# Three feed-forwards rearranged: all inner tiles first, then the down projection output by output, in 512 columns

## The reference, cut to what matters

```python
# layer 0
f = (silu(h @ w_ffn_gate) * (h @ w_ffn_up)) @ w_ffn_down
x = x + rms_norm(f, post_ffn_norm)
# layers 1 and 2
h = rms_norm_2(x, ffn_norm_g[l])
x = x + (silu(h @ ffn_w_gate[l]) * (h @ ffn_w_up[l])) @ ffn_w_down[l]
# after layer 2
return rms_norm_2(x, final_norm_g)
```

## Time and profile before

| | |
|---|---|
| median of three runs | 994.09 us |
| the profiled execution, its own time | 994.75 us |
| its span, first to last instruction | 993.0 us |
| TensorE matmul busy | 982.1 us, 99% |
| VectorE busy | 727.4 us, 73% |
| ScalarE busy | 527.6 us, 53% |
| DMA | 156.64 MB, mean 158 GB/s |
| granted TensorE clock | 9 of tenths (full) in all 40 slices |

### The profile page before, as it was taken

One profiled execution on the slowest core, in us unless ns is written; L12 is line 12 of the kernel. 1 busy time (PEld: TensorE's weight loads), 2 busy tenths in 40 slices (PEclk: granted clock), 3 DMA queues, 4 the chain that ended last, 5 costly groups with the idle time before them and its releaser, 6 DMA issues.

```text
span 993.0 us, 18707 instructions
## 1 busy us (share of the span) xinstructions
PE 982.1 (99%) x7840; PEld 895.6 (90%) x7840; DVE 727.4 (73%) x1219; ACT 527.6 (53%) x787; POOL 4.2 (0%) x11
## 2 busy tenths in 40 slices
PE   9999999999999999999999999999999999999997
PEld 8998999898989988889999898998887999899997
DVE  6978688886767997857676666788877577676666
ACT  5486564545456663556455454475446455544543
POOL 1000000000000000000000000000000000000000
PEclk9999999999999999999999999999999999999999
DMA  9744534545453322313565455443221265545531
GB/s 340 197 159 158 185 133 170 202 181 212 170 194 141 127 97 88 128 43 131 186 214 203 175 182 200 170 165 117 94 101 44 84 213 171 209 172 185 197 128 43
DMA packets 24684, 156.64 MB, mean 158 GB/s; under 512 B 2720, under 2 KB 4264, under 8 KB 7064
## 3 DMA queue, kind: packets, MB, share of 16 engines
q1 hardware_dynamic: 22320, 151.64, 42.8%
q10 hardware_dynamic: 1928, 2.49, 1.1%
q0 software_dynamic: 352, 1.31, 0.4%
HBM read 153.99 MB, written 1.44 MB: 157 GB/s over the span
## 4 chain that ended last, share of the span: by engine, by line
PE 91%; DVE 4%; ACT 2%; issue 2%; DMA 1%; SPq 0%; DVEq 0%; ACTq 0%
PE bank L489 42%; PE bank L715 21%; PE bank L717 10%; PE bank L576 2%; DVE arena L1780 1%; PE bank L1009 1%; PE bank L1014 1%; ACT w_hi L1296 1%; DVE w_lo L1798 1%; PE bank L1025 1%; PE bank L581 1%; PE bank L970 1%; DMA raw<-in_w 1%; PE bank L1233 1%; PE bank L518 1%
## 5 line engine op out<-in xcount | busy, mean ns | idle before, releaser
L1798 DVE TENSOR_TENSOR w_lo<-raw,w_hi 128x2048 fp32r<-128x2048 f32 (+3 forms) x141 | 316.9, 2250 | 103.0 <-ACT w_hi L1296 102.6
L715 PE MATMUL bank<-h_both,w_hi 128*128 128x512 f32 x912 | 323.5, 399 | 1.6 <-DVE arena L1780 1.6
L1296 ACT ACTIVATE w_hi<-raw 128x2048 fp32r<-128x2048 f32 (+4 forms) x153 | 273.2, 1787 | 34.4 <-PE bank L489 27.6
L717 PE MATMUL bank<-h_both,w_lo 128*128 128x256 f32 x912 | 256.7, 281 | 0.0
L715 PEld LDWEIGHTS bank<-h_both,w_hi 128*128 128x128 f32 x912 | 171.6, 188 | 42.9 <-DVE arena L1780 2.3
L489 PE MATMUL bank<-mix_hi,w_hi 128*128 128x256 f32 x720 | 207.0, 287 | 0.0
L489 PE MATMUL bank<-mix_lo,w_hi 128*128 128x256 f32 x720 | 204.1, 284 | 0.0
L489 PE MATMUL bank<-mix_hi,w_lo 128*128 128x256 f32 x720 | 204.1, 283 | 0.0
L717 PEld LDWEIGHTS bank<-h_both,w_lo 128*128 128x128 f32 x912 | 172.8, 189 | 0.0
L489 PE MATMUL bank<-h_both,w_hi 128*128 128x256 f32 x880 | 163.9, 288 | 0.3 <-DVE w_lo L1798 0.2
L489 PEld LDWEIGHTS bank<-h_both,w_hi 128*128 128x128 f32 x880 | 137.3, 191 | 6.2 <-issue 2.1
(11 more groups left out here) (317 smaller groups left out, 1049.3 us busy)
## 6 DMA issues: line engine op xcount, KB each, us to landing
raw<-in_w SPq DMA_DIRECT2D x136, 1024.0 KB, 4.9
raw<-in_w SPq DMA_DIRECT2D x2, 896.0 KB, 4.5
raw<-in_w SPq DMA_DIRECT2D x3, 512.0 KB, 3.6
raw<-in_w SPq DMA_DIRECT2D x2, 768.0 KB, 4.2
cst<-in_consts SPq DMA_DIRECT2D x1, 1120.0 KB, 11.0
raw<-in_first SPq DMA_DIRECT2D x4, 256.0 KB, 5.1
x<-in_first SPq DMA_DIRECT2D x4, 256.0 KB, 5.3
arena<-bias_rows ACTq DMA_DIRECT2D x4, 256.0 KB, 5.5
```

What stands on the lines that cost most here:

```text
L715: pe.matmul(to, hi(k), h_both[:, :, k, :], start=(k == 0), stop=False, skip_group_check=True)
L717: last = pe.matmul(to[:, 0, :], lo(k), h_hi[:, k, :], start=False, stop=(k == KT - 1), skip_group_check=True)
L1296: return act.activation(dst, src, ACT.Copy, **kw)
L1798: dve.tensor_tensor(w_lo[:, s, 0:n], raw[:, s, 0:n], w_hi[:, s, 0:n].bitcast(F32), ALU.subtract)\
```

## The change

A feed-forward now has two parts. First all 22 inner tiles are made and their hi and lo parts kept, side by side in one buffer (`act_both`) in the arena. Then the down products come output by output: output d takes its 22 products in order. For outputs 0 to 6 each is one matmul of 512 columns and one of 256 into a bank of their own (7, 4 and 5 in turn); output 7 keeps three of 256 into bank 6. The down weights are laid out in that order, 16 tiles to a chunk. The two sums of an output are added (`output`), and the squares of an output are made and summed as soon as it is there (`squared`, `squares`). Gate and up of the wide inner tiles use banks 0 to 3 in turn. The rounding of an inner tile (`rounded`) and its rest (`rest`) come one turn later on ScalarE and VectorE than before. The angles, the Sin and the table load for Ln and Exp move into the second part; the angles' buffers move to the mixer's. Not shown below: in `normed_residual`, outputs 0 to 6 are read from SBUF (xg) and the part sums between the halves are gone; the last norm's gains go with each output; `norm_sum` takes two addends for a half in place of three or four.

```diff
@@ -97,6 +97,15 @@
 ]
+DOWNS = KT * FT // 16
+DOWN_EVENTS = sorted([(16 * i + 16, "chunk", i) for i in range(DOWNS)] + [(FT * d + FT, "tile", d) for d in range(KT)])
+DOWN_EVENTS = [event[1:] for event in DOWN_EVENTS if event[1:] not in (("chunk", DOWNS - 1), ("tile", KT - 1))]
 def stream():
     out = []
@@ -106,10 +115,8 @@
         if l:
             out += [(l, "uq", 0, 2 * 768), (l, "ukv", 0, 1024)]
         out += [(l, "out", i, CH) for i in range(4)]
-        out += [(l, "gu", 0, CH), (l, "gu", 1, CH)]
-        for p in range(1, FT // 2):
-            out += [(l, "gu", 2 * p, CH), (l, "gu", 2 * p + 1, CH), (l, "down", p - 1, CH)]
-        out.append((l, "down", FT // 2 - 1, CH))
+        out += [(l, "gu", j, CH) for j in range(FT)]
+        out += [(l, "down", i, CH) for i in range(DOWNS)]
     return out
@@ -292,7 +300,10 @@
         xo = xg.rearrange("p k t -> p (k t)").rearrange("p (h k t) -> p h k t", h=2, k=KT)
         FF, _ = area(0, dict(gu=(2, 2, T), sg=(2, T), act=(2, T), part=(2, T), sums=(2, T)))
-        act_hi, act_lo = mix_hi[:, 0:4, :], mix_lo[:, 0:4, :]
+        act_both = nc.alloc_sbuf_tensor_at("act_both", [P, 2, FT, T], F32R, offset=arena_at + 12 * T * 4)
+        act_hi, act_lo = act_both[:, 0, :, :], act_both[:, 1, :, :]
+        assert (12 + 2 * FT) * T <= ARENA - 4096
         B1, at_products = area(0, dict(
             lx=(2, 259), lg=(2, T), glr=(T,), gk=(T,), gq=(T,), gv=(TT, T), gout=(2, T), mq=(4, T), mk=(4, T),
@@ -419,18 +430,12 @@
         WIDE = range(3, FT)
-        def gate_up_turn(j):
-            return j + sum(i < j for i in WIDE)
         def gate_up_bank(j, t=0):
...
+            return pairs((2 * (j - 3) + t) % 4 if j in WIDE else (4, 5, 7)[j])
+        def fed_bank(d):
+            return pairs((7, 4, 5)[d % 3])
         def projected(l, i):
@@ -710,7 +699,8 @@
                         for t in range(2):
                             hi, lo = tile_of(c, KT, 2 * P, t * P)
                             to = gate_up_bank(j, t)
-                            pe.wait_ge(V.sem, gate_up_read(l, gate_up_turn(j) + t - 3))
+                            if j - 2 in WIDE:
+                                pe.wait_ge(V.sem, V.at(l, ("gate", "up")[t], j - 2))
                             for k in range(KT):
                                 pe.matmul(to, hi(k), h_both[:, :, k, :], start=(k == 0), stop=False,
                                           skip_group_check=True)
@@ -718,8 +708,6 @@
                                                  skip_group_check=True)
                             last.then_inc(M.sem, M.mark(l, "gu" if t else "gate", j))
                         return
-                    if j >= 3:
-                        pe.wait_ge(V.sem, gate_up_read(l, gate_up_turn(j) - 3))
                     for t in range(2):
                         if just_come and t == 0:
                             rounded_first(gate_up_bank(j)[:, t, :], c, 2 * P, 0, 2 if c in HALVED else 1)
@@ -729,40 +717,31 @@
                             norm_sum(l, "ffn")
                     last.then_inc(M.sem, M.mark(l, "gu", j))
...
+                def down():
+                    pe.wait_ge(V.sem, V.at(l, "gu", 2))
+                    for i in range(KT * FT):
+                        d, j = divmod(i, FT)
+                        c, first, end = CHUNK[l, "down", i // 16], j == 0, j == FT - 1
+                        if i % 16 == 0:
+                            split(pe, c)
+                        if d == 0:
+                            pe.wait_ge(V.sem, V.at(l, "act", "lo", j))
+                        elif first and 3 <= d < KT - 1:
+                            pe.wait_ge(V.sem, V.at(l, "fed", "read", d - 3))
+                        hi, lo = tile_of(c, 16, P, 0)
+                        if d < KT - 1:
+                            pe.matmul(fed_bank(d), hi(i % 16), act_both[:, :, j, :], start=first, stop=False,
+                                      skip_group_check=True)
+                            last = pe.matmul(fed_bank(d)[:, 0, :], lo(i % 16), act_hi[:, j, :], start=False, stop=end,
+                                             skip_group_check=True)
+                        else:
+                            last = product(out_tile(l, "fed", d), (hi, lo), [i % 16],
+                                           [lambda k, q=q: q[:, j, :] for q in (act_hi, act_lo)],
+                                           start=first, stop=end, loose=True)
+                        if end:
+                            last.then_inc(M.sem, M.mark(l, "fed", "tile", d))
+                        elif i % 16 == 15:
+                            last.then_inc(M.sem, M.mark(l, "down", i // 16))
                 c = CHUNK[l, "gu", 0]
                 pieces = [(1, gate_up_bank(0), [(c, 2 * P, 0), (c, 2 * P, P)]),
@@ -770,11 +749,9 @@
                 as_they_come(l, "ffn", pieces[:2 if l == 0 else 1])
                 if l:
                     gate_up(1)
...
+                for j in range(2, FT):
+                    gate_up(j)
+                down()
@@ -1421,40 +1398,69 @@
                         hi_of(c + RING)
                 def silu(j):
-                    if j >= 1:
-                        act.wait_ge(V.sem, V.at(l, "act", "lo", j - 1))
                     act.wait_ge(V.sem, V.at(l, "gu", j))
                     act.activation(FF["sg"][:, j % 2, :], FF["gu"][:, j % 2, 0, :], ACT.Silu)\
                         .then_inc(A.sem, A.mark(l, "silu", j))
+                def rounded(j):
                     act.wait_ge(V.sem, V.at(l, "act", j))
-                    copy(act_hi[:, j % 4, :], FF["act"][:, j % 2, :]).then_inc(A.sem, A.mark(l, "act", "hi", j))
+                    copy(act_hi[:, j, :], FF["act"][:, j % 2, :]).then_inc(A.sem, A.mark(l, "act", "hi", j))
+                def parts(j):
+                    for t in range(2):
+                        act.wait_ge(M.sem, M.at(l, "gu" if t else "gate", j))
+                        if j - 1 in WIDE:
+                            act.wait_ge(V.sem, V.at(l, ("gate", "up")[t], j - 1))
+                        copy(FF["part"][:, t, :], gate_up_bank(j, t)[:, 1, :]).then_inc(A.sem, A.mark(l, "part", t, j))
+                def output(d):
+                    if l == 0:
+                        act.wait_ge(M.sem, M.at(l, "fed", "tile", d))
+                        copy(xg[:, d, :], fed_bank(d)[:, 1, :]).then_inc(A.sem, A.mark(l, "fed", "part", d))
+                    if l == 1 and d in (2, 4, 6):
+                        hi_of_x(l + 1, "in", f"attn{l + 1}", d // 2 - 1)
+                    if l != 1 and d:
+                        squared(d - 1)
+                def squared(d):
+                    act.wait_ge(V.sem, V.at(l, "fed", "read", d))
+                    src, name = (xg, (l, "fed")) if l == 0 else (x, (LAYERS, "final"))
+                    act.activation(sq[:, d, :], src[:, d, :], ACT.Square).then_inc(A.sem, A.mark(*name, "sq", d))
                 after(c0)
                 norm_factor(l, "ffn")
                 after(c0 + 1)
...
+                for j in range(2):
+                    silu(j)
+                    rounded(j)
+                after(c0 + 2)
+                silu(2)
+                rounded(2)
+                for j in WIDE:
+                    parts(j)
+                    after(CHUNK[l, "gu", j])
+                    if j - 1 in WIDE:
+                        rounded(j - 1)
+                    silu(j)
+                rounded(FT - 1)
+                if l == 2:
+                    ln_and_exp()
+                for kind, i in DOWN_EVENTS:
+                    if kind == "tile":
+                        output(i)
+                        continue
+                    after(CHUNK[l, "down", i])
+                    if l == 0 and i == 6:
                         act.wait_ge(V.sem, V.at("angles"))
-                        for i in range(4):
-                            last = act.activation(rope[:, i, :], rope[:, i, :], ACT.Sin)
+                        for n in range(4):
+                            last = act.activation(rope[:, n, :], rope[:, n, :], ACT.Sin)
                         last.then_inc(A.sem, A.mark("rope"))
+                        ln_and_exp()
+                if l != 1:
+                    squared(KT - 2)
             def block1():
                 l, lru = 0, B1["lru"]
@@ -2388,25 +2373,48 @@
                 def added(j):
-                    after_a(l, "silu", j - 2)
-                    after_v(l, "act", j - 2)
                     for t, name in enumerate(("gate", "up")):
                         after_a(l, "part", t, j)
                         tt(FF["sums"][:, t, :], gate_up_bank(j, t)[:, 0, :], FF["part"][:, t, :], ALU.add, l, name, j)
                     after_v(l, "up", j)
+                    after_a(l, "silu", j - 2)
+                    after_v(l, "act", j - 2)
                     tt(FF["gu"][:, j % 2, :, :], FF["sums"], wide(rstd[:, :], 2), ALU.mult, l, "gu", j)
-                def feed(j):
```

(68 more changed lines are left out.)

171 lines of the change are left out of this document (26 added, 145 removed).

## The result

The changed kernel took 987.08 us (median of 6 runs, 986.06 to 988.36) against 994.19 us for the kernel before beside it (6 runs): ratio 0.9928, 95% interval 0.9919 to 0.9938. That is 7.1 us less where 5.6 were forecast, and 0.2 us under the range. The six runs form two groups: 986.20, 986.11 and 986.06, and 987.98, 988.36 and 987.96. The mean granted clock was 0.998 or 0.999 in all six, so the clock doesn't part them. The profiled execution is of the first group (986.20 us, span 984.4).

The account below looks back on a forecast made before the run. TensorE, busy 99% of the span, was taken as the bound; gains of 3.0 (down), 2.0 (layer 0's wait), 0.5 (end of layer 0) and 0.1 (last norm) sum to 5.6 us, giving 988.5 us, range 987.3 to 991.2.

Parts of the forecast that it names:

- What would show it: Signs against: wide matmuls waiting mid first part for VectorE or a lo split, output 0's last products waiting, clock leaving 1.00.
- Down products: Outputs 0 to 6: two matmuls a tile instead of three save 6.6 ns on 462 tiles, 3.0 us; bounds 0 to 3.4.
- The isolated gap's rule: Down tiles: a fixed cost of 2.5 ns per instruction, 1.2 us in all; with the pair's rival, chance together 0.06.
- The wait in layer 0: First wide tiles of layer 0: TensorE's waits for VectorE to read a bank, 2.12 us, go; 2.0 us counted as gained.
- No stall in 22 tiles in a row: Gate-up part: about 6 us of room stand ahead of any stall of the successive wide tiles: 0.
- none from inner tiles to down: Output 0 wants inner tile 21 last, with 0.8 us of room before TensorE would wait: 0.
- none in the down part: Second part: VectorE's and ScalarE's work, with the angles, Sin and table load, fits the room without stalling TensorE: 0.
- the slower rival: First part: VectorE's loop becomes longer than TensorE's 5.65 us a tile, such as 17 us lost, 1005.6 us; chance 0.05.
- The end of layer 0: Layer 0's last norm step: Ln no longer waits for VectorE's part sums, 0.5 us gained; bounds 0 and 0.6.
- The last norm: Final norm: the square of tile 7 no longer waits for VectorE's sum behind a part sum, 0.1 us gained.
- more than forecast: Case of more gain, from steps priced at nothing or a smoother first part, down to 986 us; chance 0.07.

Follow-up runs that it names:

- e3: The changed kernel with each down tile of outputs 0 to 6 made by three matmuls of 256 columns instead of one of 512 and one of 256: 991.93 us.
- e7: The changed kernel with down products of layers 0 and 2 fed from the gate and up activations instead of the kept inner tiles: 985.67 us, one execution.
- e2: The changed kernel with six banks in turn instead of four for wide gate and up, so no pause at inner tile 5 of layer 0: 987.49 us.
- e4: The changed kernel with one wait at the start of each layer's down part, for TensorE's own last gate-up product: 987.09 us.

## Why the prediction missed, step by step

Two terms failed: the price of a down pair, and the first part of layer 0, which was priced at one pace for its row. None of the signs under "What would show it" that would make the forecast wrong came, and yet the time left the range.

**Down products.** Right in mechanism, mis-sized by a third: 6.6 ns a tile forecast, 8.7 to 9.0 measured (0.3597 to 0.3510; e3 0.3600), 4.0 to 4.1 us and not 3.0. The term failed in taking 0.3534 us, the price of a gate-up pair in one stretch, for the down pair, which takes 0.3510; e7 shows that the operand makes the difference. The step said that its operand lies in another buffer, but used that for the lower bound only; it put an upper bound of 3.4 us from reading accuracy alone. A better bound was in the trace of the kernel before. Two stretches of two wide tiles each in its layer 1, the first an early one, the second like all later ones:

```profile
492.37:503.52 11.15, 11.15 (x66) 9.79 (x65) 8.75 (x9) 5.98 (x8) 0.00 (x0) 1.00 0.48 159
509.27:520.58 11.31, 11.31 (x66) 9.82 (x65) 7.29 (x10) 5.67 (x8) 0.00 (x0) 1.00 0.55 187
```

11.15 us against 11.31 (and 11.11 in layer 2, under e2) for the same instructions: the price has a spread of up to 1.8%, and one case was taken for it. With 11.11/32 = 0.3472 the upper bound would have been 462 x (0.3600 - 0.3472) = 5.9 us. The isolated gap's rule of the Trainium skill ("TensorE: Matmul & The Clock Gate", section "Back-to-back issue gap") gives 2.5 ns a tile by its fixed cost and lay further off: the trace disagrees with 8.7 to 9.0 ns.

**The wait in layer 0.** The chain worked said 151.6 for the sum of tile 3's gate against TensorE at 151.57; measured were 151.2 and 151.23, and the pause was 0.15 us. The 2.0 us were right. What failed was to take a wait's price as its length: behind the pause the row ran 1.7 us faster (105.83 us against 107.41 and the pause of 0.15) in the profiled execution, which is of the group at 986.1, three of six. In the other group the gain is 994.19 - 988.0 = 6.2 us, against 5.6 forecast; the difference is the down step (+1.0) less the two items of 0.3 and 0.2 below. That group lies inside the range. That the median of six left it rests on how many executions happened to take the fast pace, which nothing in the prediction or here explains. e2 shows the same kernel without the pause: 987.5.

**No stall in 22 tiles in a row, none from inner tiles to down, none in the down part.** Right: apart from the 0.15 us at tile 5 the wide pairs and the down pairs of the profile after have no idle time before them. But "0" left out that two wide tiles in each of layers 1 and 2 had run at the fast pace before and no longer do, 0.3 us lost together. VectorE as the bound, the slower rival, didn't come: 84 us of work in 107.4.

**The end of layer 0.** 0.5 forecast, 1.51 - 1.06 = 0.45 in the Ln and 0.5 to the next layer's first product. **The last norm.** +0.1 forecast, -0.1 measured: VectorE's sum starts 0.31 us after the start of the last product before (985.36 to 985.67) and 0.32 after (976.69 to 977.01), so there was nothing to gain; too small to be tested.

**The range.** Its lower end, 987.3, left out the faster pace and had 0.4 us of room for the down pair where 1.0 was needed. Two paces of one instruction stream were not among the cases; "more than forecast" had 0.07.

## What to carry to other kernels

Price a matmul form from more than one stretch of the trace, and look at the spread between stretches before taking their mean: here it was up to 1.8% between two rows of the same instructions, as much as the forecast effect of the edit (0.3600 to 0.3534). When TensorE is the bound and never idle, a pause of 0.04 to 0.3 us in or ahead of a row of 100 us was worth 1.6 to 2 us here, as a gain where it led to the fast pace and as a loss where it took it away, so a result near such a margin should be read from several executions and their groups, not from one. The kernel with six banks and no wait lay within 1 us in its four executions (987.4 to 988.2). The one with the wait did so too in its first four (983.3), and then gave 989.0 in four of five, so four executions on one chip prove little; no run showed how to make it keep the first.

## What the runs showed of the hardware

At a granted clock of 1.00 (2.4 GHz), rows of one 512-column and one 256-column matmul with their weight loads have three steady paces: 0.3467, 0.3511 and 0.3534 us a pair. The first and last are paces that an unbroken row of pairs kept for 105 and 107 us, and that passed from one group of products into the next (e7: from gate-up into down). A pause of 0.04 to 0.3 us could change the pace or leave it. The middle pace came with the kept inner tiles in the arena as operand, whichever pace the row ahead had, and a pause didn't change it (e4). In the variants of the changed kernel rows without a pause always went at the slow pace: the wide parts of layers 1 and 2 in all eleven profiles that have no wait there. In the kernel before the pace changed without a pause too, across down chunks of three matmuls a tile: slow to fast and back to slow in layer 2 at 826.33 and 843.18.
